# Gated linear attention: decay arguments of one direction from matrix products, both sides multiplied on VectorE, levels in groups of three

## The chip, the cores and the metric

The kernel runs on one core of one Trainium2 chip. Its time is the device time of one execution, in microseconds (us); three runs are given by their median.

## What is computed

The reference is a stack of two networks on 256 context and 256 latent tokens of width 1024. The part that the change touches is the gated linear attention mixer of the first layer: four heads of key width 128 and value width 256, run once forward and once backward over the 512 tokens.

```
q, k, v, g, a = split(h @ w_in)
logit = einsum('blzr,zrd->zbld', a.reshape(b, l, 2, 16), w_a2) + b_a2
log_a = log_sigmoid(logit) / 16
cum   = cumsum(log_a)                       # within a chunk
attn[i, j] = sum_d q[i,d] k[j,d] exp(cum[i,d] - cum[j,d])   for j <= i
o = attn @ v + (q * exp(cum)) @ state
state = state * exp(last) + (k * exp(last - cum))^T @ v
y = (rms_norm(o_forward + o_backward) * silu(g)) @ w_out
```

Since the decay differs in each key feature d, `attn` is no plain product. The kernel splits a chunk of 128 tokens by levels 64, 32, 16, 8, 4, 2, 1: at level s, queries and keys on the two sides of an edge between two runs of s tokens are scaled to that edge, which gives a plain product for the pairs that the edge parts. The exponents are differences between a running sum of log gates and its value at the edge.

## The kernel before, in words

Each stage is a block with one written-out program per engine (TensorE, ScalarE, GpSimd, VectorE, and SyncE for the loads), tied together by semaphores: `wait_ge` holds back the engine's whole queue, in order. Nothing is scheduled by a tool, so the order of the code is the order of the work. `b.stage()` begins a stage, with a barrier between stages.

`gla_project` makes queries, keys, values, gate and the log gates. Its TensorE program is long products in three parts (each weight slab is rounded on ScalarE, and the remainder is made on GpSimd). After eight short products (`logits`), ScalarE makes the softplus (`log_gate`, L1144), and VectorE forms the log gates and their running sums (`cum`), four forward and four backward, by scans.

`gla_core` is the stage of the change. For each of the four heads h it goes through levels n = 0 to 6 (sizes 64 to 1), q = 7h + n:

- VectorE makes the forward difference and GpSimd the backward one (`make_diff`, L1243), ScalarE takes four exponentials of 128x256 into `ak` and `bq` (`factors`, L1356 and L1357), VectorE multiplies the key side (L1516) and GpSimd the query side (L1440).
- TensorE multiplies them (`scores(h, n + 1)`, L1267, four products of 128x128), and VectorE takes the part that belongs to the level out of the bank with a mask (`take_score`, L1480). `scores(h, 0)` is the diagonal.
- Beside it run the state (`turn_keys` L1279, `addends` L1289, `states` L1502), the output of the head before (`outputs`, L1303 and L1308) and the sums of its squares (`add_squares`, L1062).
- TensorE also works off 40 *vector steps* (`ada_step`, L466; ten per head, spread by `STEPS`) that have nothing to do with the mixer: they multiply a stationary vector with two slabs of 512 KB each, which SyncE streams into a ring of four slabs. A load waits until the slab four places earlier has been used (`weights_used`), so at most two steps are loaded ahead.

A value in `[...]` of the order below is the list of semaphores that the instruction waits for.

## Time and profile before

| | us |
|---|---|
| median of 3 runs (2658.5 to 2662.23) | 2661.91 |
| profiled execution, its own time | 2668.94 |
| profiled execution, span | 2667.2 |
| `gla_core` in it | about 203.2 to 370.4 |
| TensorE busy over the span | 2481.5 (93%) |
| VectorE busy | 1360.4 (51%) |
| ScalarE busy | 1195.9 (45%) |
| GpSimd busy | 617.8 (23%) |

The span is from the first to the last instruction of the profiled execution, which took 0.3% more than the median of the three runs. The stage in question is 6% of it. A busy share over the whole span says little here, because stages have different limits; the heads of `gla_core` have to be read one by one. TensorE's float32 products appear as two records each, so a score product of four instructions shows as x8.

### The profile page before, as it was taken

To read this page: it belongs to the slowest core of one execution; us is meant where nothing else is said; L and a number is where in the kernel's file an instruction comes from. 1 tells how busy PE (TensorE), PEld (TensorE's weight loads), DVE (VectorE), ACT (ScalarE), POOL (GpSimd) and SP (SyncE) were. 2 spreads that over 40 slices of the span, in tenths; PEclk is the share of its full clock that TensorE was granted. 3 is DMA by queue.
4 is the path that set the end of the run, shared out by engine and by line. 5 is a ranking of instruction groups with operands and counts; after the bars stand their busy time and mean duration, and the time that the engine had idled before them with its cause. 6 is when DMAs were issued, how large, how long until landed. Compare 5 with 4: busy or idle time off the path is not lost. (4 is left out here: it accounts for less than half of the span.)

```text
span 2667.2 us, 35079 instructions
## 1 busy us (share of the span) xinstructions
PE 2481.5 (93%) x13744; PEld 1969.8 (74%) x13744; DVE 1360.4 (51%) x2129; ACT 1195.9 (45%) x2029; POOL 617.8 (23%) x376
## 2 busy tenths in 40 slices
PE   5997889999998998999997999999999979999988
PEld 3784457888888888578996767577767858768778
DVE  2207657433445666347665534552566444454665
ACT  1833334422327433455554345564366234565363
POOL 1437620000006434110001442003301116403310
PEclk8998999999999999988998999999999989999999
DMA  7236852333324332645764231222222323334333
GB/s 229 79 87 210 294 171 79 112 96 94 102 72 135 103 87 64 243 152 149 199 188 112 63 93 46 68 57 75 72 65 71 87 64 95 108 91 116 86 102 114
DMA packets 416683, 302.12 MB, mean 113 GB/s; under 512 B 10306, under 2 KB 388776, under 8 KB 416520
## 3 DMA queue, kind: packets, MB, share of 16 engines
q1 hardware_dynamic: 415408, 299.45, 38.3%
q8 instruction: 110, 1.80, 0.3%
q10 hardware_dynamic: 1112, 0.44, 0.1%
q14 instruction: 53, 0.43, 0.1%
HBM read 298.80 MB, written 1.05 MB: 112 GB/s over the span
## 5 line engine op out<-in xcount | busy, mean ns | idle before, releaser
L207 POOL TENSOR_TENSOR weights_lo<-wslots,weights_hi 128x1024 fp32r<-128x1024 f32 x158 | 386.6, 2455 | 868.7 <-ACT weights_hi L197 622.3
L197 ACT ACTIVATE weights_hi<-wslots 128x1024 fp32r<-128x1024 f32 x398 | 418.2, 1054 | 292.7 <-PE psum L260 235.0
L260 PE MATMUL psum<-input_hi,weights_hi 128*128 128x512 f32 (+1 forms) x1400 | 501.0, 358 | 4.5 <-PEq L831 1.8
L260 PE MATMUL psum<-input_hi,weights_lo 128*128 128x512 f32 (+1 forms) x1400 | 489.1, 349 | 0.0
L260 PE MATMUL psum<-input_lo,weights_hi 128*128 128x512 f32 (+1 forms) x1400 | 488.3, 349 | 0.0
L207 DVE TENSOR_TENSOR weights_lo<-wslots,weights_hi 128x1024 fp32r<-128x1024 f32 x240 | 296.4, 1243 | 187.7 <-ACT weights_hi L197 187.4
L260 PEld LDWEIGHTS psum<-input_hi,weights_hi 128*128 128x128 f32 x1400 | 264.5, 189 | 44.7 <-issue 7.5
L260 PEld LDWEIGHTS psum<-input_lo,weights_hi 128*128 128x128 f32 x1400 | 263.4, 188 | 39.2 <-issue 3.4
L260 PEld LDWEIGHTS psum<-input_hi,weights_lo 128*128 128x128 f32 x1400 | 263.7, 188 | 38.1
L260 PE MATMUL psum<-ffn_hidden_hi,weights_hi 128*128 128x512 f32 (+1 forms) x512 | 172.8, 338 | 0.0
L260 PE MATMUL psum<-ffn_hidden_hi,weights_lo 128*128 128x512 f32 (+1 forms) x512 | 172.5, 337 | 0.0
L260 PE MATMUL psum<-ffn_hidden_lo,weights_hi 128*128 128x512 f32 (+1 forms) x512 | 171.6, 335 | 0.0
L2304 DVE RECIPROCAL head_rstd<-head_rstd 128x512 f32<-128x512 f32 (+1 forms) x32 | 94.4, 2951 | 104.1 <-ACT head_rstd L2296 104.1
L3138 PE MATMUL psum<-input_hi,weights_hi 128*128 128x512 f32 (+1 forms) x384 | 139.4, 363 | 2.7 <-PEq L3225 2.7
L466 PE MATMUL psum<-wslots,ada_c 128*32 128x512 f32 x576 | 111.1, 640 | 27.2 <-DMA wslots<-ada_w 23.5
L3138 PE MATMUL psum<-input_lo,weights_hi 128*128 128x512 f32 (+1 forms) x384 | 133.0, 346 | 0.0
L3138 PE MATMUL psum<-input_hi,weights_lo 128*128 128x512 f32 (+1 forms) x384 | 132.7, 345 | 0.0
L279 PE MATMUL psum<-input_hi,weights_hi 128*128 128x512 f32 (+1 forms) x216 | 83.6, 387 | 48.2 <-DVE input_lo L684 44.6
L260 PEld LDWEIGHTS psum<-ffn_hidden_hi,weights_hi 128*128 128x128 f32 x512 | 96.8, 189 | 10.2 <-issue 0.2
L260 PEld LDWEIGHTS psum<-ffn_hidden_hi,weights_lo 128*128 128x128 f32 x512 | 96.5, 189 | 10.6
L260 PEld LDWEIGHTS psum<-ffn_hidden_lo,weights_hi 128*128 128x128 f32 x512 | 96.1, 188 | 11.2 <-issue 0.2
L997 ACT ACTIVATE ffn_hidden<-psum 128x512 f32<-128x512 f32 (+1 forms) x64 | 31.3, 490 | 135.9 <-PE psum L260 123.1
(449 smaller groups left out, 4864.7 us busy)
## 6 DMA issues: line engine op xcount, KB each, us to landing
wslots<-w_in SPq DMA_DIRECT2D x132, 512.0 KB, 3.9
wslots<-ffn_w SPq DMA_DIRECT2D x128, 512.0 KB, 4.1
wslots<-ada_w SPq DMA_DIRECT2D x96, 512.0 KB, 4.9
wslots<-ssd_w_in SPq DMA_DIRECT2D x49, 512.0 KB, 4.0
wslots<-w_ada SPq DMA_DIRECT2D x48, 512.0 KB, 4.6
wslots<-gla_w_in SPq DMA_DIRECT2D x25, 512.0 KB, 3.8
wslots<-w_br SPq DMA_DIRECT2D x24, 512.0 KB, 3.6
wslots<-ssd_w_out SPq DMA_DIRECT2D x16, 512.0 KB, 4.8
```

Of the source, the lines that this page charges most:

```text
L197: act.activation(self.part(self.whi_r, n), self.slot(n), ACT.Copy)\
L207: engine.tensor_tensor(self.part(self.wlo_r, n), self.slot(n), self.part(self.whi, n), ALU.subtract)\
L260: ins = pe.matmul(out_of(self.bank(g)), l, r, start=first and i == 0, stop=last and i == len(pairs) - 1, skip_group_check=not (first and l ...
L279: ins = pe.matmul(self.bank(g + j)[:, a:e], l, r, start=k == 0 and i == 0, stop=k == KD - 1 and i == 2, skip_group_check=True)
L466: ins = pe.matmul(b.psum[32 * q:32 * q + 32, bank, :], b.ada_c[:, blk, k, :], b.slot(n)[:, 0, q % 2 * 512:(q % 2 + 1) * 512], start=k == 0 ...
L997: act.activation(hid[:, j % NH, :], b.bank(g)[:, a:e], ACT.Relu).then_inc(b.reads_out(g), 1)
L2304: dve.reciprocal(r, r).then_inc(b.tick("dve_step"), 1)
L3138: ins = pe.matmul(b.bank(g)[:, a:e], w, u, start=x == 0, stop=x == len(pairs) - 1, skip_group_check=True)
```

## The change

- `gla_project`: the bias goes into the product as a row of ones (33 rows instead of 32), so the copy with bias (L1139) goes. The forward log gates stay as they are, tokens on partitions, with no scan; only the four backward ones are scanned. VectorE builds `sums`, nine 0/1 matrices of 128x128, one for each level and two for the chunk's ends, from a table of masks of 768 KB and one of 128 KB that are loaded at the stage's start.
- `gla_core`, forward side: the log gates are split into a rounded part and a remainder (`round_gates` on ScalarE, `split_gates` on VectorE, once per head). TensorE multiplies them with `sums` (`arguments(G, ...)`): three groups G of a head, each with three matrices (group 0 holds level 64 and the two ends, group 1 levels 32, 16, 8, group 2 levels 4, 2, 1), each in four *fills*, one per chunk of 128 tokens, of two products of 128x384. ScalarE takes one exponential of each fill (48 in all) into `decay`.
- `gla_core`, backward side: GpSimd makes all 32 differences (`make_diffs`), ScalarE the exponentials (`exponents_back`).
- VectorE multiplies both sides (`make_sides`, two instructions of 128x512 per level). GpSimd keeps the query factors of the chunk's ends and the small vectors.
- A level's sides wait for all four fills of its group. `STEPS` and the places of states, outputs and turns on TensorE are new; `addends(h, 2)` moves from the next head into its own.

```diff
+GLA_SIZES = [P // 2] + LEVELS
+GLA_SLOTS = len(GLA_SIZES) + 2
...
+                    sp.dma_start(wa[RB:RB + 1, z, :], d["gla_b_a2"][0, z:z + 1, :])\
+                        .then_inc(b.tick("gate_weights_in", 16), 16)
+                sp.dma_start(pairs[:], d["c_gla_masks"].rearrange("p (z n k) -> p z n k", z=2, k=P))\
+                    .then_inc(b.tick("pairs_in", 16), 16)
+                sp.dma_start(runs[:, 0:2, :], d["c_causal"]).then_inc(b.tick("pairs_in", 16), 16)
...
+                        pe.wait_ge(b.sem("log_gate_made"), b.nth("log_gate_made", n - 3))
+                    left, right = (wa[:, 1, i], aT[:]) if z else (aT[:, i], wa[:, 0, :])
+                    pe.matmul(b.psum[:, 4 + n % 4, :], left, right, start=True, stop=True)\
+                        .then_inc(b.tick("logit_ready"), 1)
...
-                    act.activation(lx[:, n % 2, :], b.psum[:, 4 + n % 4, :], ACT.Identity,
-                                         bias=column(b, C_GLAB, n)).then_inc(b.tick("logit_read"), 1)
...
-                for n in range(2 * GH):
-                    z, h = n // GH, n % GH
+                for n in range(2 * TT):
                     dve.wait_ge(b.sem("softplus_ready"), b.nth("softplus_ready", n + 1))
-                    dve.scalar_tensor_tensor(le[:, n % 2, :], lx[:, n % 2, :], 0.0, le[:, n % 2, :],
-                                                       ALU.min, ALU.subtract).then_inc(b.tick("dve_step"), 1)
+                    x = le[:, n % 2, :]
+                    ins = dve.scalar_tensor_tensor(x if n >= TT else b.H2[:, n, :], b.psum[:, 4 + n % 4, :], 0.0, x,
+                                                   ALU.min, ALU.subtract)
+                    if n >= TT:
+                        ins.then_inc(b.tick("dve_step"), 1)
+                        dve.wait_ge(b.sem("dve_step"), b.all("dve_step"))
+                        ins = dve.tensor_tensor_scan(b.H2[:, n, ::-1], reset[:], le[:, n % 2, ::-1], 0.0, ALU.mult, ALU.add)
+                    ins.then_inc(b.tick("log_gate_made"), 1)
...
+                step(dve.tensor_tensor(sums_r[:, 3:GLA_SLOTS, :], pairs[:, 0], blocks[:], ALU.mult))
...
-        STEPS = [1, 1, 1, 2, 2, 2, 1]
...
+        STEPS = (2, 1, 1, 2, 1, 1, 2)
+        EARLY = 2
...
+                    for c in range(first, last):
+                        f = G * FILLS + c
+                        if f >= 2:
+                            pe.wait_ge(b.sem("exponents_taken"), b.nth("exponents_taken", f - 1))
+                        for part, side in enumerate((gates_hi_r, gates_lo_r)):
+                            ins = pe.matmul(b.psum[:, ARG[c % 2], 0:WIDE * P], side[:, c, h * GDK:(h + 1) * GDK],
+                                            sums_r[:, g * WIDE * P:(g + 1) * WIDE * P], start=part == 0, stop=part == 1)
+                        ins.then_inc(b.tick("arguments_made"), 1)
...
+                scores(0, 0)
+                arguments(0, 0, FILLS)
+                vectors(0, 0, 0, EARLY)
                 for h in range(GH):
...
+                    G = h * GROUPS
+                    arguments(G + 1, 0, 1)
+                    if h:
+                        scores(h, 0)
+                        vectors(h, 0, 0, 1)
+                    arguments(G + 1, 1, 2)
+                    if h:
+                        outputs(h - 1)
+                    arguments(G + 1, 2, 3)
+                    scores(h, 1)
+                    if h:
+                        vectors(h, 0, 1, STEPS[0])
+                    arguments(G + 1, 3, 4)
+
+                    scores(h, 2)
+                    turn_keys(h, 0)
+                    arguments(G + 2, 0, 1)
+                    vectors(h, 1, 0, STEPS[1])
+
+                    scores(h, 3)
+                    turn_keys(h, 1)
+                    arguments(G + 2, 1, 2)
+                    vectors(h, 2, 0, STEPS[2])
+                    if h:
+                        sum_squares(h - 1)
+
+                    arguments(G + 2, 2, 3)
+                    scores(h, 4)
+                    vectors(h, 3, 0, STEPS[3])
+                    addends(h, 0)
+                    arguments(G + 2, 3, 4)
+
+                    scores(h, 5)
+                    addends(h, 1)
+                    arguments(G + 3, 0, 1)
+                    vectors(h, 4, 0, STEPS[4])
+                    if (h, 4) in TURN:
+                        turn_vectors(TURN[h, 4])
+
+                    scores(h, 6)
+                    addends(h, 2)
+                    arguments(G + 3, 1, 2)
+                    vectors(h, 5, 0, STEPS[5])
+
+                    arguments(G + 3, 2, 3)
+                    scores(h, 7)
+                    vectors(h, 6, 0, STEPS[6])
+                    arguments(G + 3, 3, 4)
+                    if (h, 6) in TURN:
+                        turn_vectors(TURN[h, 6])
...
+                def exponents(G, first, last):
+                    if G == GH * GROUPS:
+                        return
+                    if first == 0:
+                        buffer_free(G)
+                    for c in range(first, last):
+                        act.wait_ge(b.sem("arguments_made"), b.nth("arguments_made", G * FILLS + c + 1))
+                        act.activation(decay[:, G % 2, 0, :, c * P:(c + 1) * P],
+                                       b.psum[:, ARG[c % 2], 0:WIDE * P].rearrange("p (n k) -> p n k", k=P), ACT.Exp, scale=INV)\
+                            .then_inc(b.tick("exponents_taken"), 1)
...
+                            early, late = pairs(x, SIZES[0 if g == 0 else 3 * g - 2 + slot])
+                            act.activation(early, early, ACT.Exp, scale=INV)
+                            ins = act.activation(late, late, ACT.Exp, scale=-INV)
+                    ins.then_inc(b.tick("exponents_back"), 1)
...
+                    exponents(G + 1, 0, 2)
+                    exponents_back(G + 1, 0)
+                    if h:
+                        copy_output(h - 1)
+                    exponents(G + 1, 2, 4)
+                    exponents_back(G + 1, 1)
+                    exponents_back(G + 1, 2)
+                    vectors(h, 0)
+                    if h == 0:
+                        round_gates(1)
+                        round_gates(2)
+                        round_gates(3)
+                    else:
+                        square_output(h - 1)
+                    exponents(G + 2, 0, 1)
+                    copy_keys(h, 0)
+                    exponents_back(G + 2, 0)
...
+                    make_diffs(G + 1)
+                    pool.wait_ge(b.sem("exponents_taken"), b.nth("exponents_taken", (G + 1) * FILLS))
+                    pool.wait_ge(b.sem("exponents_back"), b.nth("exponents_back", (G + 1) * WIDE))
+                    if h >= 2:
+                        pool.wait_ge(b.sem("output_made"), b.nth("output_made", 2 * (h - 1)))
+                    for z in range(2):
+                        x = decay[:, G % 2, z, QUERY_SLOT, :]
+                        edge = x.rearrange("p (c r) -> p c r", r=P)[:, :, (P - 1) * (1 - z)]
+                        pool.tensor_copy(el[:, h % 2, z, :], edge).then_inc(b.tick("edge_copied"), 1)
+                        pool.tensor_tensor(qhT[:, h % 2, z, :], x, qT[:, h, :], ALU.mult).then_inc(b.tick("query_hat"), 1)
+                    if h:
+                        pool.wait_ge(b.sem("vectors_copied"), b.nth("vectors_copied", h))
+                        ada_finish(b, pool, h, vec)
+                    make_diffs(G + 2)
+                    make_diffs(G + 3)
...
+                    for z in range(2):
+                        if z == 0:
+                            dve.wait_ge(b.sem("exponents_taken"), b.nth("exponents_taken", (G + 1) * FILLS))
+                        else:
+                            dve.wait_ge(b.sem("exponents_back"), b.nth("exponents_back", G * WIDE + level_slot(n) + 1))
+                        x = decay[:, G % 2, z, level_slot(n), :].rearrange("p (n i s) -> p n i s", i=2, s=s)
+                        dve.tensor_tensor(crossed(sides[:, q % 2], z, s), x, crossed(qk[:, h], z, s), ALU.mult)\
+                            .then_inc(b.tick("sides_ready"), 1)
...
+                split_gates(0)
+                make_masks()
                 for h in range(GH):
                     for n in range(NL):
-                        q = h * NL + n
-                        if q + 1 < Q:
-                            make_diff(dve, 0, q + 1)
-                        if n == 3:
-                            key_hats(h)
-                        dve.wait_ge(b.sem("factors_ready"), b.nth("factors_ready", q + 1))
-                        x = ak[:, q % 2, :]
-                        dve.tensor_tensor(x, x, kT[:, h, :], ALU.mult).then_inc(b.tick("key_side"), 1)
-                        if q == 0:
-                            make_masks()
+                        if h or n:
+                            make_sides(h, n)
+                        else:
+                            take_score(0, 0)
+                            make_sides(0, 0)
                         if n == 0 and h:
                             take_score(h - 1, NI - 1)
-                        take_score(h, n)
-                        if n == 6:
-                            states(h, 0)
-                        if n in (0, 1) and h:
-                            states(h - 1, n + 1)
+                        if n or h:
+                            take_score(h, n)
+                        if n == 0:
+                            key_hats(h)
+                            if h == 0:
+                                for x in range(1, GH):
+                                    split_gates(x)
+                        if n in (4, 5, 6):
+                            states(h, n - 4)
...
```

How this moves the rows on the engines is shown at three places.

**TensorE, second head, around the product of level 32.** Before (`gla_bq` and `gla_ak` are the two sides; L466 is a vector step):

```order
L466 MATMUL psum<-wslots,ada_c 32x512
L1267 MATMUL psum<-gla_bq,gla_ak 128x128 [waits query_side,key_side,score_taken]
L1267 MATMUL psum<-gla_bq,gla_ak 128x128 x3
L466 MATMUL psum<-wslots,ada_c 32x512 [waits weights_in_3]
L466 MATMUL psum<-wslots,ada_c 32x512
```

Of the changed kernel, the same place (`gla_sums` are the 0/1 matrices, `weights_hi` and `weights_lo` hold the split log gates, `gla_sides` both sides; L468 is the vector step):

```order
L468 MATMUL psum<-wslots,ada_c 32x512 [waits weights_in_0]
L468 MATMUL psum<-wslots,ada_c 32x512
L1321 MATMUL psum<-gla_sums,weights_hi 128x384 [waits exponents_taken]
L1321 MATMUL psum<-gla_sums,weights_lo 128x384
L1334 MATMUL psum<-gla_sides 128x128 [waits sides_ready,score_taken]
L1334 MATMUL psum<-gla_sides 128x128 x3
```

The last fill of the group now stands directly ahead of the first score product that is made from this group.

**TensorE, same head, around the product of level 4,** of the changed kernel (L1365 are `addends`):

```order
L468 MATMUL psum<-wslots,ada_c 32x512 [waits weights_in_0]
L468 MATMUL psum<-wslots,ada_c 32x512
L1365 MATMUL psum<-gla_v,gla_kh 128x256 [waits key_hat_copied,output_copied]
L1365 MATMUL psum<-gla_v,gla_kh 128x256
L1321 MATMUL psum<-gla_sums,weights_hi 128x384 [waits exponents_taken]
L1321 MATMUL psum<-gla_sums,weights_lo 128x384
L1334 MATMUL psum<-gla_sides 128x128 [waits sides_ready,score_taken]
L1334 MATMUL psum<-gla_sides 128x128 x3
```

Here too the last fill (of group 2) and the first product of its levels are neighbours.

**VectorE, start of the stage.** Before:

```order
L1243 TENSOR_TENSOR gla_diff<-gla_cum 128x512 x2
L1516 TENSOR_TENSOR gla_ak<-gla_ak,gla_qk 128x512 [waits factors_ready]
L1463 TENSOR_SCALAR gla_masks<-half_ones 128x128 [waits masks_in]
L1465 TENSOR_TENSOR gla_masks<-gla_state 128x768
L1476 TENSOR_TENSOR gla_score<-psum,gla_diag 128x512 [waits score_made,masks_ready]
```

Of the changed kernel:

```order
L1638 TENSOR_TENSOR weights_lo<-h,weights_hi 128x4x128 [waits gates_rounded]
L1629 TENSOR_SCALAR gla_masks<-half_ones 128x128 [waits masks_in]
L1631 TENSOR_TENSOR gla_masks<-gla_state 128x768
L1662 TENSOR_TENSOR gla_score<-psum,gla_diag 128x512 [waits score_made,masks_ready]
L1652 TENSOR_TENSOR gla_sides<-gla_decay,gla_qk 128x4x2x64 [waits exponents_taken]
L1652 TENSOR_TENSOR gla_sides<-gla_decay,gla_qk 128x4x2x64 [waits exponents_back]
L1675 TENSOR_TENSOR gla_khT<-gla_decay,gla_qk 128x512 [waits exponents_back]
L1675 TENSOR_TENSOR gla_khT<-gla_decay,gla_qk 128x512
L1638 TENSOR_TENSOR weights_lo<-h,weights_hi 128x4x128 [waits gates_rounded] x3
L1652 TENSOR_TENSOR gla_sides<-gla_decay,gla_qk 128x8x2x32 [waits exponents_taken]
```

The sides of level 64 moved behind the masks, and the sides of level 32 stand behind three remainders, whose rounded parts ScalarE makes only after the exponentials of group 1.

## Rows read from the trace of the kernel before

**Rows 1.** Windows: the project stage's long part, then the four heads of the core.

```profile
core 0: us, PE busy (x) PEld busy (x) DVE busy (x) ACT busy (x) POOL busy (x), PEclk, DMA share, GB/s
...
120.00:203.00 83.00, 82.90 (x356) 66.42 (x354) 5.75 (x6) 33.61 (x43) 31.18 (x13) 1.00 0.29 83
...
203.00:249.20 46.20, 30.50 (x161) 15.18 (x160) 31.59 (x31) 17.67 (x47) 34.11 (x23) 0.78 0.63 221
249.20:287.00 37.80, 33.04 (x227) 19.51 (x225) 26.59 (x30) 15.50 (x43) 25.72 (x21) 1.00 0.79 268
287.00:324.20 37.20, 33.74 (x226) 19.34 (x225) 25.23 (x30) 15.49 (x43) 27.00 (x22) 1.00 0.80 288
324.20:370.40 46.20, 39.68 (x278) 25.57 (x276) 24.98 (x31) 14.39 (x40) 20.90 (x21) 1.00 0.77 258
```

**Rows 2.** Waits from 230 to 371: engine, line, releaser, us, times, longest.

```profile
POOL gla_bq L1440 <- ACT gla_bq L1357: 37.0, 13, 8.2
PEld psum L466 <- DMA wslots<-ada_w: 33.4, 30, 2.5
...
PE psum L1267 <- DVE gla_ak L1516: 2.4, 2, 1.2
```

**Rows 3.** Timeline of TensorE in the third head: start, duration, line, [idle before].

```profile
287.98 1.06 PE L1267 MATMUL psum<-gla_bq,gla_ak 128*128 128x128 f32 x8
288.87 0.60 PE L489 MATMUL psum<-ident,ada_flat 128*128 128x128 f32 x4
289.31 1.03 PE L1289 MATMUL psum<-gla_v,gla_kh 128*128 128x256 f32 x4
290.26 1.06 PE L466 MATMUL psum<-wslots,ada_c 128*32 128x512 f32 x8
...
295.42 1.06 PE L1303 MATMUL psum<-gla_score,gla_v 128*128 128x128 f32 x8
...
299.98 1.06 PE L466 MATMUL psum<-wslots,ada_c 128*32 128x512 f32 x8
...
302.15 0.60 PE L1279 MATMUL psum<-ident,gla_khT 128*128 128x128 f32 x4
302.68 1.06 PE L466 MATMUL psum<-wslots,ada_c 128*32 128x512 f32 x8
305.15 2.22 PE L466 MATMUL psum<-wslots,ada_c 128*32 128x512 f32 x8 [1.40 <-DMA wslots<-ada_w]
307.30 1.16 PE L1267 MATMUL psum<-gla_bq,gla_ak 128*128 128x128 f32 x8
308.29 0.60 PE L1279 MATMUL psum<-ident,gla_khT 128*128 128x128 f32 x4
...
315.15 1.84 PE L1062 MATMUL psum<-ones,gla_sq 128*128 128x1 f32 x16
316.93 2.19 PE L466 MATMUL psum<-wslots,ada_c 128*32 128x512 f32 x12
```

**Rows 4.** Timeline of the stage's start: masks on VectorE, first two level products.

```profile
209.73 1.84 DVE L1465 TENSOR_TENSOR gla_masks<-gla_state 128x768 uint8<-128x768 f32 x1
209.87 1.13 PE L1267 MATMUL psum<-gla_bq,gla_ak 128*128 128x128 f32 x8 [2.75 <-POOL gla_bq L1440]
...
214.79 2.05 PE L1267 MATMUL psum<-gla_bq,gla_ak 128*128 128x128 f32 x8 [3.79 <-DVE gla_ak L1516]
```

**Rows 5.** Groups by line, 230 to 371: busy us, mean ns | idle before.

```profile
L1480 DVE COPY_PREDICATED gla_score<-gla_masks,psum 128x512 f32<-128x512 uint8 x24 | 17.5, 731 | 32.0 <-PE psum L1267 31.8
...
L1356 ACT ACTIVATE gla_ak<-gla_diff 128x256 f32<-128x256 f32 x44 | 18.3, 416 | 46.5 <-PE psum L1267 23.9 <-DVE gla_diff L1243 19.8 <-POOL gla_diff L1243 2.9
...
L482 ACT ACTIVATE ada_flat<-psum 128x512 f32<-128x512 f32 x5 | 3.0, 597 | 27.2 <-PE psum L466 27.2
```

**Rows 6.** Timeline of VectorE and ScalarE in the third head.

```profile
302.45 1.76 DVE L1516 TENSOR_TENSOR gla_ak<-gla_ak,gla_qk 128x512 f32<-128x512 f32 x1
...
308.50 0.74 DVE L1480 COPY_PREDICATED gla_score<-gla_masks,psum 128x512 f32<-128x512 uint8 x1 [2.03 <-PE psum L1267]
308.58 0.44 ACT L1356 ACTIVATE gla_ak<-gla_diff 128x256 f32<-128x256 f32 x1 [1.32 <-PE psum L1267]
...
310.03 0.69 DVE L1516 TENSOR_TENSOR gla_ak<-gla_ak,gla_qk 128x512 f32<-128x512 f32 x1 [0.22 <-ACT gla_bq L1357]
```

376 lines of the change are left out of this document (208 added, 168 removed).

## The prediction

> **What bounds the kernel now.** I read first the windows of the stage, because over the span TensorE is 93% busy and tells nothing of one stage. In the long part of the project stage TensorE is busy for 82.90 of 83.00 us [rows 1]: what the change saves or adds there on the other engines is hidden behind it, or does not count. In the core the heads take 46.2, 37.8, 37.2 and 46.2 us, the last with the output of its own behind it [rows 1]. VectorE and GpSimd are busy for only 25 to 27 us of the two middle heads. Then the list of waits: GpSimd waits long for ScalarE (37.0 us), which costs nothing as long as TensorE does not wait for it. TensorE's queue of weight loads waits for the slabs of the vector steps (33.4 us in 141 us, some 9 per head) and hardly for a side of the scores (2.4 us) [rows 2]. So a middle head is TensorE's own work plus waits for slabs.
>
> TensorE's work follows from starts in the timeline of the third head [rows 3]: a score product 0.9 to 1.0 us (288.87 less 287.98, 308.29 less 307.30), a turn of keys 0.53, of vectors 0.45, addends 0.95, the outputs 4.6 (299.98 less 295.42), squares 1.8, a vector step 1.06. One head has 8 products (7.8), 2 turns (1.1), 3 addends (2.9), outputs, squares, a turn of vectors and 10 steps (10.6): 29.2 us. Against 37.2 that leaves 8.0 of waiting.
>
> The slabs explain most of it. The ring holds two steps, so a step cannot run before its slots, freed by the step two places earlier, are filled again. Step 3 of this head ends at 301.04, step 5 at 307.30 [rows 3]: 6.26 us, of which 1.06 are its own, so a refill takes about 5.2 us. I use 5.0 to 5.2. Where three pairs of steps stand close together (after levels 8, 4 and 2), the second of two has 2.7 us behind it and waits 2.4. Adding up this rule over the order of before gives 2.4 + 2.4 + 0.3 + 1.8 = 6.9 us of a head, most of the 8.0.
>
> **What the change adds to TensorE.** Per head 12 fills of two products of 128x384. The nearest row is the project stage, where a 128x512 product of the same rounded kind takes 83.00 / 356 = 0.233 us [rows 1]; three quarters of it is 0.175, so 0.35 a fill and 4.2 us a head. The bounds: as short as one of the eight records of a score product (0.12 each, 0.25 a fill, 3.0 a head), as long as the 512 columns (0.47, 5.6 a head). I take 0.35. Work per head: 33.4 us.
>
> **What it does to the waits for slabs.** The steps are now spread as 2, 1, 1, 2, 1, 1, 2, and one of the first two stands ahead of the outputs. I went through the new order with the same durations and the same refill of 5.0. Step 6 stands directly behind step 5 (squares, a fill and a product lie ahead of step 5): between the end of step 4 and step 6 lie 4.2 us, wait 0.9. Step 9: 0.3. Step 10: a fill, a product and step 9 lie between, 2.7, wait 2.3. The others have their 5 us. Sum 3.5, so the new order saves about 3.5 of 6.9, and the 1.1 that TensorE waited for other things goes too. Bounds: 0 and the old 7.
>
> **What it adds as a wait.** This term decides. In the shown order of TensorE the last fill of group 1 stands directly ahead of level 32's product, and the last fill of group 2 directly ahead of level 4's, and these products wait for `sides_ready`. Between the neighbours lies a chain over two engines, and nothing on TensorE can pass it: end of the fill to ScalarE 0.3 (308.29 to 308.58 [rows 6]); one exponential of 128x384 from a bank, 0.5 (between 0.416 for 256 columns and 0.597 for 512 [rows 5]); VectorE's two multiplications, 0.69 each when GpSimd is quiet (310.03 [rows 6]); 0.1 back. Together 2.3 us, twice per head: 4.6. Queued behind the product on TensorE are the turn of keys, the next fill and the next step, so the whole head moves. The slabs land meanwhile, but the steps that lack them (6 and 10) are not the ones behind these stalls, so little is given back. Bounds: with the exponential at 0.42 and hops of nothing it is 1.8 each; with both multiplications at 1.76, as beside a GpSimd instruction [rows 6], 4.4 each.
>
> A third place is short: the outputs wait for `take_score` of the head before, which on VectorE stands behind the two sides of level 64, which wait for the head's last fill. From that fill: 0.3 + 0.5 + 0.7 + 0.7 + 0.73 [rows 5] + 0.2 = 3.1, with GpSimd's query factors beside it up to 3.8. TensorE has a fill, a product, a step and a fill in front, 2.8. I take 0.6.
>
> The other levels: VectorE needs 0.73 + 1.4 = 2.1 between two sides, 3.1 where a state goes between; TensorE has 2.9 to 5 us of its own there. Nothing. ScalarE needs per head 12 x 0.5 + 7 x 0.83 + some 5 for copies, 17 of 42 us; GpSimd 8 differences and two products, about 14. Neither bounds.
>
> **Middle heads:** 33.4 + 3.5 + 4.6 + 0.6 = 42.1, against 37.8 and 37.2: +4.3 and +4.9.
>
> **Last head:** no fills for a next group (4 x 0.35 less), 40.7 to the end of its steps; then the last vectors are copied and turned (1.5), the outputs 4.6 and their copy 0.8: 47.6 against 46.2, +1.4. That `addends(h, 2)` moved is in it.
>
> **First head.** It is a chain of levels before: the products of levels 64 and 32 start at 209.87 and 214.79, after waits of 2.75 and 3.79, and the second already takes 2.05 instead of 1.06, with the mean granted clock of the head at 0.78 [rows 1, 4], that is partly at 1.2 GHz. Afterwards VectorE begins with the masks, whose table lands some 4 us into the stage; they end at 210 to 211 (209.73 + 1.84 before [rows 4]), then the diagonal and the sides of level 64, so that this product starts at about 213.5. Level 32 stands behind ScalarE's exponential of the last fill (0.5), four of 256 columns (1.7), three roundings (0.6 each), the last remainder (0.7) and two sides (1.4), with product, fill and hop 7.7 us: 221.3, 6.5 later than before. From there I count TensorE's order with its waits: 2.9, 3.3, then 8.7 (two steps short of slabs, and the stall), 3.4, 3.7 and 6.2, which ends at 249.5 against 249.2. The price is small because the old head was also slow in its middle; with some products at half clock I take +2. Bounds -3 and +6.
>
> **Project stage:** 0. ScalarE loses eight copies, VectorE four scans and gains some 25 short instructions, all beside the busy TensorE; 0.9 MB more on the queue of loads needs 3 us where it waits for GpSimd anyway.
>
> **Sum:** 2 + 4.3 + 4.9 + 1.4 = +12.6 us. On the profiled execution's 2668.94 that is 2681.5; on the median of the runs, 2661.91, it is 2674.5.
>
> **Rivals.** (A) *VectorE is slowed by GpSimd in the chain.* The same multiplication takes 0.69 alone and 1.76 in other places [rows 6]. If GpSimd's differences lie beside the chains, each of the four multiplications takes 1.07 more, and the outputs' chain 1.1: +5.4 a head, 22 in all, 2696. For it: VectorE has twice the multiplications. Against: GpSimd works a third of the head, and after the last fills its differences should be done. The Trainium skill (SBUF — State Buffer, on the shared port pair) says that a VectorE instruction with two SBUF inputs and a GpSimd instruction that reads SBUF exclude each other and the later one waits for all of the other; by that rule the sum would be (A)'s wherever the two meet, and the 12.6 where they don't. The trace agrees as to size, 1.76 against 0.69.
>
> (B) *The slabs are the only bound, and the new stalls hide in them.* If every slab lands during a stall, the 3.5 go too: heads of 38.6, in all 2 + 0.8 + 1.4 - 2.1 = +2.1, 2664, no change to be measured.
>
> (C) *Faster.* As (B), and the first head is no longer a chain of levels, since three levels come ready at once. It stands 8.7 us above a middle head today. If it falls to 40, -6, and with (B)'s others at +0.1, the time is 2656. It decides only if the product of level 32 starts before about 213; the wait for three roundings speaks against it.
>
> (D) *The fills don't run as assumed*, because changing between rounded and full products costs, or the clock falls in the stalls. At 0.47 a fill it is +5.8 in all, 2680, inside the range of the likeliest.
>
> **How the numbers follow.** Likeliest, with (D): 0.55, 2667 to 2684. (A) 0.15; (B) 0.13; (C) 0.17. A measurement of this kernel can tell about 0.2%, 5.3 us. Slower: 0.55 of the likeliest less 0.02, and (A): 0.68. Same: (B) and 0.02: 0.15. Faster: (C), 0.17. The range 2657 to 2700 leaves out half of (C) and the end of (A).
>
> **What would show it.** In the new profile: L1321 at about 0.17 us each; TensorE idle for 2 to 2.5 us before L1334 twice a head, released by VectorE's `gla_sides`; waits for `ada_w` at 3 to 5 us a head instead of 7 to 9; heads of about 42 us; VectorE's L1652 mostly at 0.7; level 32's first product near 221. It would be wrong if the score products after the last fills showed no idle time, if L1652 took over 1.2 us because of its crossed access (its runs are as short as one element, which no row of before shows on VectorE with two such operands), or if the ring refilled in 4 us.

## The result and the profile after

The changed kernel takes **2684.64 us** (median of 4 runs, 2682.94 to 2690.47), the kernel before beside it 2662.07 (4 runs). The ratio is 1.0078, 95% interval 1.0055 to 1.0102: the medians stand 22.6 us apart, where +12.6 was forecast. The time lies inside the stated range of 2657 to 2700, and 0.6 us over the upper end of the likeliest part (2684). The profiled execution took 2682.94 us, its span is 2681.2.

The windows of the four heads of the changed kernel, cut where each head's diagonal product starts, the first 0.9 us ahead of it at the stage's begin, and the last where its output ends (start:end, length, busy time and count on TensorE, its weight loads, VectorE, ScalarE, GpSimd, then granted clock, DMA share, GB/s):

```profile
203.90:254.07 50.17, 35.03 (x202) 20.05 (x203) 24.65 (x35) 19.39 (x45) 18.24 (x17) 0.93 0.59 205
254.07:298.46 44.39, 38.77 (x250) 24.39 (x249) 17.92 (x30) 14.64 (x38) 12.65 (x14) 0.92 0.68 237
298.46:342.76 44.30, 37.67 (x249) 24.62 (x249) 18.98 (x30) 15.09 (x38) 13.08 (x15) 0.96 0.69 236
342.76:392.10 49.34, 42.04 (x283) 27.68 (x282) 19.71 (x31) 13.67 (x35) 10.05 (x14) 0.97 0.73 238
```

Against [rows 1] the heads are 4.0, 6.6, 7.1 and 3.1 us longer, 20.8 in all. So the core holds nearly the whole difference of the medians. (The two profiled spans differ by only 14.0 us: behind the core the profile of before took 2294.0 us and this one 2286.3, in stages that differ from one execution to the next.) VectorE and GpSimd have less to do than before in both middle heads, and the granted clock of these, 1.00 before, is 0.92 and 0.96.

The waits of the changed kernel from 230 to 392 us (engine, line, releaser, us, times, longest), beside [rows 2]:

```profile
PEld psum L468 <- DMA wslots<-ada_w: 26.7, 21, 2.4
PE psum L1334 <- DVE gla_sides L1652: 14.5, 7, 2.1
PE psum L468 <- DMA wslots<-ada_w: 8.9, 13, 1.5
```

The slabs cost less than before (TensorE's own waits for them were 14.6 us in the 141 us of before, and are 8.9 in 162). The new line is the second: seven waits of 2.07 us for the two sides of a level. The timeline of TensorE in the third head shows one of them, around level 32's product, and the pair of steps behind level 8's:

```profile
308.28 0.45 PE L1321 MATMUL psum<-gla_sums,weights_hi 128*128 128x384 f32 x1
308.56 0.34 PE L1321 MATMUL psum<-gla_sums,weights_lo 128*128 128x384 f32 x1
310.97 2.05 PE L1334 MATMUL psum<-gla_sides 128*128 128x128 f32 x8 [2.07 <-DVE gla_sides L1652]
312.81 1.06 PE L1346 MATMUL psum<-ident,gla_khT 128*128 128x128 f32 x4
313.52 0.67 PE L1321 MATMUL psum<-gla_sums,weights_hi 128*128 128x384 f32 x1
313.99 0.51 PE L1321 MATMUL psum<-gla_sums,weights_lo 128*128 128x384 f32 x1
...
321.51 1.91 PE L468 MATMUL psum<-wslots,ada_c 128*32 128x512 f32 x12
324.18 1.05 PE L468 MATMUL psum<-wslots,ada_c 128*32 128x512 f32 x4 [0.75 <-DMA wslots<-ada_w]
```

ScalarE and VectorE meanwhile (same kernel, same place):

```profile
308.94 0.49 ACT L1474 ACTIVATE gla_decay<-psum 128x384 f32<-128x384 f32 x1 [1.81 <-PE psum L1321]
...
309.53 1.29 DVE L1652 TENSOR_TENSOR gla_sides<-gla_decay,gla_qk 128x512 f32<-128x512 f32 x2 [5.83 <-ACT gla_decay L1474]
```

Read together: the second product of the last fill starts at 308.56, and the next of its kind could have started 0.17 later, at 308.73; the exponential runs from 308.94, the two multiplications from 309.53 to 310.82, and the product starts at 310.97. That is the forecast chain link by link, 2.2 us from 308.73 against the forecast 2.3. (The profile lets the fill end at 308.90, so it shows 2.07 of idle time.) What the forecast did not have is behind it: the product takes 2.05 in place of 1.05, the turn of keys 1.06 in place of 0.60, the next fill 0.67 and 0.51 in place of 0.42 and 0.34. TensorE stood still for 2.07 us and then ran at the lower of its two levels (1.2 GHz; the granted clock is 0.51 from 310.97 to 314.42). From 310.97 to the next step at 314.42 pass 3.45 us; the same four groups take 1.85 at full clock (305.02 to 306.87 in run 1 below), so the clock costs 1.6.

Such stalls are not the only place. In the second head the clock is low behind level 32's product (0.56 from 266.11 to 270.00) and once more where no such stall stands ahead, behind the squares and level 8's product:

```profile
276.64:280.30 3.66, 3.56 (x15) 0.53 (x16) 0.00 (x0) 0.00 (x0) 0.00 (x0) 0.53 0.55 186
```

There two steps run that lack slabs, so what it costs can't be read off.

A middle head taken apart by the starts in TensorE's timeline (time from each group to the next, its own waits for slabs counted to the steps; us; worked out from all rows of the third head):

| | before | forecast | after |
|---|---|---|---|
| scores | 7.9 | 7.8 | 8.6 |
| turns, addends, outputs, squares | 10.6 | 10.8 | 9.9 |
| ten steps with slab waits | 17.6 | 14.1 | 15.1 |
| twelve fills | 0 | 4.2 | 6.6 |
| other waits | 1.1 | 5.2 | 4.1 |
| head | 37.2 | 42.1 | 44.3 |

### The profile page after: what moved, and what is told of

Same layout as the page of the kernel before. It is cut to its first block and busy times, and to the rows that moved or that the text cites. A ratio compares the mean times of both kernels' runs of the same rounds, so it can differ in the third digit from the quotient of the medians.

```text
span 2681.2 us, 35271 instructions
## 1 busy us (share of the span) xinstructions
PE 2486.5 (93%) x13840; PEld 1977.0 (74%) x13840; DVE 1338.5 (50%) x2154; ACT 1191.9 (44%) x2001; POOL 561.0 (21%) x353
## 3 DMA queue, kind: packets, MB, share of 16 engines
HBM read 299.72 MB, written 1.05 MB: 112 GB/s over the span
## 5 line engine op out<-in xcount | busy, mean ns | idle before, releaser
L262 PE MATMUL psum<-input_hi,weights_hi 128*128 128x512 f32 (+1 forms) x1400 | 500.5, 357 | 4.4 <-PEq L833 1.8
L262 PE MATMUL psum<-input_hi,weights_lo 128*128 128x512 f32 (+1 forms) x1400 | 488.3, 349 | 0.0
L262 PE MATMUL psum<-input_lo,weights_hi 128*128 128x512 f32 (+1 forms) x1400 | 487.3, 348 | 0.0
L262 PEld LDWEIGHTS psum<-input_hi,weights_hi 128*128 128x128 f32 x1400 | 263.8, 188 | 44.8 <-issue 7.8
L262 PEld LDWEIGHTS psum<-input_lo,weights_hi 128*128 128x128 f32 x1400 | 263.8, 188 | 39.2 <-issue 3.4
L262 PEld LDWEIGHTS psum<-input_hi,weights_lo 128*128 128x128 f32 x1400 | 263.9, 188 | 38.1
L262 PE MATMUL psum<-ffn_hidden_hi,weights_hi 128*128 128x512 f32 (+1 forms) x512 | 172.0, 336 | 0.0
L262 PE MATMUL psum<-ffn_hidden_hi,weights_lo 128*128 128x512 f32 (+1 forms) x512 | 171.7, 335 | 0.0
L262 PE MATMUL psum<-ffn_hidden_lo,weights_hi 128*128 128x512 f32 (+1 forms) x512 | 170.8, 334 | 0.0
L468 PE MATMUL psum<-wslots,ada_c 128*32 128x512 f32 x576 | 104.5, 631 | 21.4 <-DMA wslots<-ada_w 17.6
L262 PEld LDWEIGHTS psum<-ffn_hidden_lo,weights_hi 128*128 128x128 f32 x512 | 96.1, 188 | 11.2 <-issue 0.2
L262 PEld LDWEIGHTS psum<-ffn_hidden_hi,weights_hi 128*128 128x128 f32 x512 | 96.6, 189 | 10.2 <-issue 0.2
L262 PEld LDWEIGHTS psum<-ffn_hidden_hi,weights_lo 128*128 128x128 f32 x512 | 96.1, 188 | 10.6
```

The source lines that it names most:

```text
L262: ins = pe.matmul(out_of(self.bank(g)), l, r, start=first and i == 0, stop=last and i == len(pairs) - 1, skip_group_check=not (first and l ...
L468: ins = pe.matmul(b.psum[32 * q:32 * q + 32, bank, :], b.ada_c[:, blk, k, :], b.slot(n)[:, 0, q % 2 * 512:(q % 2 + 1) * 512], start=k == 0 ...
```

## The experiments

The runs of one kernel lie some 15 us apart (the kernel before beside runs 9 to 12: 2657.44 to 2672.6), and the stages behind the core, which no edit touches, take 2279.6 to 2299.8 us in the 14 profiles. The medians of the kernel before beside the runs below are 2665.87 (runs 1 to 4), 2666.36 (5 to 8) and 2667.28 (9 to 12), 4 to 5 us above the 2662.07 of its four runs beside the changed kernel. Against these medians the changed kernel stands 17 to 19 us higher, not 22.6. Beside the ratio, a second measure is therefore given: the length of the core in the profile, from the first diagonal product to the first product of the next stage that reads the squares (`gla_stat`). It is 169.05 us in the profile of before and 190.09 in that of the changed kernel (204.79 to 394.88), +21.0. Two profiles of the kernel before agree in it to 0.3 (run 12). A core figure below is of one profile, and "less" is against the changed kernel where nothing else is named.

**1. The last fill of group 1 earlier.**

```diff
-                    arguments(G + 1, 2, 3)
+                    arguments(G + 1, 2, 4)
                     scores(h, 1)
                     if h:
                         vectors(h, 0, 1, STEPS[0])
-                    arguments(G + 1, 3, 4)
```

> Edit: the changed kernel, with the last fill of group 1 one product and one vector step earlier, ahead of level 64's product. Theory T (stalls count in full, and the low clock behind level 32's product comes from the stall): the 2.07 us of idle time before that product fall to 0 to 0.3, the product takes 1.05 in place of 2.05, and the three later heads are 4 us shorter each, the first about unchanged: about 2684.6 - 12 = 2672.5 us. Rival S (slab waits take over what a stall frees): waits for ada_w rise from 5 to 8 or 9 us a head, the time falls by under 4 us, above 2680. Rival C (the low clock there is not the stall's doing): idle time goes, the product stays at 2.05, about -6, 2678.5.

Measured: 2675.43 us, ratio 1.0038 (1.0023 to 1.0053); core 178.99, 11.1 less than the changed kernel. Middle heads 40.28 and 41.57. Level 32's product of the third head, in this kernel:

```profile
305.02 1.13 PE L1334 MATMUL psum<-gla_sides 128*128 128x128 f32 x8 [0.36 <-DVE gla_sides L1651]
```

The wait is 0.36 and the product at full clock in all three later heads. Three times 1.71 of idle time went. Of the other 6 us of the 11.1, some 3 are clock (1.6 each in the second and the last head; the third loses as much as before, at another place); the rest is small pieces: steps that wait 0.2 to 0.6 less a head, the fill that now follows another fill, 0.5 in the first head. Theory T holds, and S and C fall: the freed time was not taken by the slabs, and the low clock behind this product went with the stall. The third head still has a granted clock of 0.96, now behind the stall of level 4, whose product takes 1.29.

**2. The last fill of group 2 earlier.** The same edit two levels on: `arguments(G + 2, 2, 4)` ahead of `scores(h, 4)`, and the call behind `addends(h, 0)` removed.

> Edit: the changed kernel, with the last fill of group 2 ahead of level 8's product, two vector steps and one pair of addends, so that these cover the chain to level 4's product. Theory T: 2.07 us of idle time less in each of the four heads and no change of clock, since the product behind this stall was already at 1.13: -8, 2676.5 us. Rival S: under -3, above 2681.5, because steps 7 and 8 then wait for slabs.

Measured: 2674.43, ratio 1.0032 (1.0008 to 1.0055); core 177.36, 12.7 less. That is more than the 8.3 of four stalls. Most of the rest is clock (1.6 us each in the second and the last head, behind level 32's product), in a place where I had not expected it. Level 32's products, whose stall is untouched here:

```profile
264.64 1.13 PE L1334 MATMUL psum<-gla_sides 128*128 128x128 f32 x8 [2.07 <-DVE gla_sides L1651]
...
304.22 1.43 PE L1334 MATMUL psum<-gla_sides 128*128 128x128 f32 x8 [2.07 <-DVE gla_sides L1651]
```

So the same stall of 2.07 us is followed by the low clock in one head (304.22, then 1.06 for the turn) and not in the others. In the changed kernel, with two stalls in a head, all three later heads lost clock. With one stall (this run and the one ahead of it) one middle head of two did, and with none, below, neither.

**3. Both earlier.**

> Edit: both of the other two, the last fill of group 1 ahead of level 64's product and the last of group 2 ahead of level 8's. Theory T: the gains add, -20, 2664.5 us, with middle heads of 38.3 and waits for ada_w still at 5 us a head. Rival S: they don't add, since the ring of slabs then bounds (10 steps of at least 2.6 us plus bunching): middle heads of 41 and more, above 2672. Rival V (VectorE's chain of levels takes over): no idle time released by a fill's chain, but by sides elsewhere, VectorE busy over 85% of a head.

Measured: 2663.58, ratio 0.9995 (0.998 to 1.001); core 170.44, 19.65 less. The two middle heads:

```profile
250.00:287.76 37.76, 35.20 (x249) 23.29 (x249) 17.96 (x30) 14.53 (x38) 12.64 (x14) 1.00 0.77 273
287.76:326.34 38.58, 36.33 (x250) 23.25 (x250) 19.03 (x30) 14.88 (x38) 13.08 (x15) 1.00 0.77 273
```

The clock is 1.00, and 19.65 of the 21.0 us that the change added to the core are gone with two lines of TensorE's program. In the last head the clock is still low once, over the last turn and part of the outputs (0.96 over that head). The twelve fills take 5.6 us here, 0.47 each, in place of 6.6. S and V fall.

**4. The roundings and remainders of heads 1 to 3 later in the first head.** ScalarE's `round_gates(1)` goes behind `copy_keys(h, 0)`, 2 and 3 behind `copy_keys(h, 1)`; on VectorE:

```diff
                             key_hats(h)
-                            if h == 0:
-                                for x in range(1, GH):
-                                    split_gates(x)
+                        if h == 0 and 0 < n < GH:
+                            split_gates(n)
```

In the changed kernel the three remainders stood ahead of level 32's sides on VectorE, and behind three roundings:

```profile
217.63 3.19 DVE L1638 TENSOR_TENSOR weights_lo<-h,weights_hi 128x512 fp32r<-128x512 f32 x3 [1.57 <-ACT weights_hi L1457]
220.74 1.28 DVE L1652 TENSOR_TENSOR gla_sides<-gla_decay,gla_qk 128x512 f32<-128x512 f32 x2
```

> Edit: the changed kernel, with the roundings and remainders of heads 1 to 3 moved behind level 32 to level 8 of the first head, so that they don't stand ahead of level 32's sides. Theory T: VectorE's three remainders (3.2 us from the first to the last) and ScalarE's roundings (1.65) leave the chain to level 32's first product; it starts 3 us sooner, near 219 on the clock of the profile, and the time falls by 3, 2681.5 us, all in the first head. Rival: the low clock of this head stays as it is and something else of the chain comes last (GpSimd's differences, the exponentials), under -1, 2684.

Measured: 2688.39, ratio 1.0089 (1.0059 to 1.0118); core 188.10, 2.0 less, the first head 0.8 less. The product does start 2.8 us sooner after the head's begin, but the time does not follow: theory T's 3 us are not there, and the rival's "under 1" fits the first head. VectorE, and then GpSimd, of this kernel show why it gains little:

```profile
215.23 2.35 DVE L1676 TENSOR_TENSOR gla_khT<-gla_decay,gla_qk 128x512 f32<-128x512 f32 x2
218.13 2.62 DVE L1653 TENSOR_TENSOR gla_sides<-gla_decay,gla_qk 128x512 f32<-128x512 f32 x2 [0.54 <-ACT gla_decay L1474]
...
226.09 0.69 DVE L1639 TENSOR_TENSOR weights_lo<-h,weights_hi 128x512 fp32r<-128x512 f32 x1 [4.69 <-ACT weights_hi L1457]
226.69 1.28 DVE L1653 TENSOR_TENSOR gla_sides<-gla_decay,gla_qk 128x512 f32<-128x512 f32 x2
```
```profile
217.72 3.93 POOL L1581 TENSOR_TENSOR gla_decay<-h 128x512 f32<-128x512 f32 x3 [1.28 <-DVE gla_khT L1676]
```

Two multiplications that take 1.28 alone take 2.62 beside GpSimd's three differences: rival (A)'s mechanism, for once, in the only head where the two engines meet in a chain. The Trainium skill (SBUF — State Buffer, section on the two separate sides) says that such a pair excludes each other for a whole instruction. The trace agrees in size: the pair of multiplications takes 1.34 longer, and one of GpSimd's three differences takes 1.31. And at 226.09 the remainder now waits for its late rounding and holds level 16's sides. The queue was moved, not removed.

**5. The steps one at a time, stalls kept.** Of the ten steps, one stands after the diagonal, one in the middle of the outputs, one behind them, and one after each level:

```diff
                        ins.then_inc(b.tick("output_made"), 1)
+                        if h < GH - 1:
+                            vectors(h + 1, 1 + vt, 0, 1)
...
-        STEPS = (2, 1, 1, 2, 1, 1, 2)
+        STEPS = (1,) * 10
...
```

> Edit: the changed kernel with its ten vector steps of a head one at a time (after level 128's product, in the middle of the outputs, behind them, then after each level's product) and no pair of steps left; the last fills of groups 1 and 2 stay where the change put them, so both stalls of 2.07 us stay. Theory T (slab waits of some 4 to 5 us a head come from steps that stand close together, a refill being 5.1 us, and add to the stalls): waits for ada_w fall under 1.5 us a head, middle heads from 44.3 to 41, the time to 10 us over the kernel before. Rival S (the ring's rate, not the bunching, sets the waits): under 1 us a head, 20 us over the kernel before.

Measured: 2672.11, ratio 1.0031 (1.0012 to 1.005); core 183.75, 6.3 less. The profiled execution was its slowest (2692.55). The third head is 40.97 long, with no wait for slabs, as theory T said. The second is 44.52: it waits 1.3 us for a slab once, and the clock is low twice, behind the squares (the step at 282.09 takes 2.51 to the next start in place of 1.00) and behind level 4's stall (the product takes 1.67, the addends 1.35 in place of 0.68). Behind its stall at level 32 the product takes 1.13, at full clock. In the third head the waits for slabs were worth what was expected; in the second the clock and one late slab took all of it back.

**6. Steps, fills and start together.**

> Edit: the steps one at a time as in the spread kernel, both last fills ahead of the product before theirs, and the roundings and remainders of heads 1 to 3 later in the first head. Theory T: work of a head 29.2 + 12 fills at 0.44 = 34.5, no stall but 0.4, slab waits under 1: middle heads of 35.5 to 36, against 37.8 with both fills ahead alone; the time 12 to 16 us under the kernel before, ratio 0.995. Rival V (VectorE's and ScalarE's chain of levels then sets the pace): idle time before the scores at other levels, heads of 37 and more, no better than both fills ahead alone.

Measured: 2646.52, ratio 0.9936 (0.9913 to 0.996); core 151.53. Middle heads 34.35 and 35.02, the first 39.76. Better than expected, and V falls. What I had not expected is the first head, 6.4 us shorter than in run 3 (46.17): the third and fourth step now stand where TensorE waits for levels 64 and 32, in place of behind them.

**7. What a fill's second product costs.** On run 3, each fill is one product in place of two. The kernel leaves out the remainder's part of the forward arguments:

```diff
-                        for part, side in enumerate((gates_hi_r, gates_lo_r)):
+                        for part, side in enumerate((gates_hi_r,)):
...
```

> Edit: both last fills ahead, and each fill made of one product in place of two; left out is the remainder's part of the forward arguments. It measures what a fill's second product costs on the path. Theory T (TensorE's work is the head's length; a fill's second product has a pitch of 0.17 to 0.18 us): 12 x 0.175 = 2.1 us a head, -8 against both fills ahead alone. Rival S (the slabs take over what TensorE saves): the waits for ada_w grow by as much, under -3.

Measured: 2664.21, ratio 0.9992 (0.9976 to 1.0008), no less than run 3. In the profile the core is 164.70, 5.7 less than run 3; the fills take 3.5 us a head in place of 5.6 (the 2.1 expected), of which 0.35 come back as a longer wait before level 32 (0.71) and some as slab waits. The 5.7 us are not seen in the time. The two ratios differ by 0.0003, 0.8 us, with some 6 us either way: that leaves T's 8 just outside and S's 3 inside, while the core lies between them, so this run does not decide.

**8. Run 3 with the later roundings.**

> Edit: both last fills ahead, and the roundings and remainders of heads 1 to 3 later in the first head; the steps stay in pairs. It tells in the combined kernel the share of the start from that of the steps. Level 32's first product starts 2.8 us sooner after the head's begin, as in the start kernel alone, but levels 16 and 8 then wait for VectorE's sides, so the first head gains 0.8 and the time stands 0 to 2 us under both fills ahead alone. Rival: the gain stays in full, -3.

Measured: 2667.78, ratio 1.0008 (0.9993 to 1.0023); core 168.89, 1.5 less than run 3. The time is as expected, but the gain is not where it was expected: the first head takes 46.33 against 46.17, and the last is 1.8 us shorter, where in run 3 the outputs ran at low clock and here they don't. The start by itself is worth nothing.

**9. The kernel before, with its steps one at a time.** The same placing of the steps in the old order; nothing else of the change.

> Edit: the kernel BEFORE the change, with its ten vector steps of a head one at a time (one after level 128's product, one in the middle of the outputs, one ahead of the squares, and so on), nothing else of the change. It tells what the new scheme of arguments is worth once both orders are free of waits for slabs. Theory T (a head is TensorE's own work plus slab waits): 29.2 of work and 1 to 2 left of slab waits, middle heads 31 to 32 against 37.5, the time 18 to 22 us under the kernel before (ratio 0.992 to 0.993), level with or better than the spread form of the changed kernel. Rival V (the old scheme's chain of a level over GpSimd, ScalarE and VectorE cannot go faster than some 5 us a level): idle time of 1 us and more before the score products, heads of 35 to 36, the time 5 to 10 us under the kernel before, and the new scheme keeps an advantage.

Measured: 2655.98, ratio 0.9958 (0.9939 to 0.9977); core 156.90, 12.2 less than before. Neither theory: the middle heads, 37.05 and 33.38, did not reach 31 to 32, but no chain of a level stood in their way either (idle time outside the steps 0.2 and 1.2 us). The first head still has 8.5 us of waits for the sides of levels 64, 32 and 16. The second lacks slabs twice (2.4 us), and behind the squares and the second of these waits the clock is low, with no stall of a chain ahead (0.53 from 279.30 to 282.90; 0.95 over the head). The third head:

```profile
284.83:318.22 33.39, 32.18 (x229) 19.62 (x225) 25.57 (x30) 15.54 (x43) 26.65 (x22) 1.00 0.89 308
```

The DMA share is 0.89 at 308 GB/s. The head's ten steps need 20 slabs of 512 KB, 10.5 MB, and at 308 GB/s that is 34 us. That the ring's own rate is the next bound is likely and not shown: four of the ten steps are stretched, to 1.4 to 1.9 us, but a share of 0.89 is not full, and no run has another ring.

**10. The steps one at a time and both fills ahead, roundings left.**

> Edit: the changed kernel with the steps one at a time and both last fills ahead, but the roundings and remainders of heads 1 to 3 where the change put them. Against the run that had all three it tells what the start is worth once steps fill its waits. Theory T: level 32's first product waits 2.8 us longer, of which the steps before it hide part; the first head 41 to 42.5 in place of 39.8, the time 1.5 to 2.5 us over the kernel with all three. Rival (the 6.6 us by which that first head was shorter came from the start edit after all): first head near 46, +6.

Measured: 2640.27, ratio 0.9904 (0.9878 to 0.993); core 151.40, the same as run 6. The first head is 38.99, not longer. So the 6.4 us of that head came from the steps, and the edit of the start gave nothing; both the theory's 1.5 to 2.5 and the rival's 6 were wrong. One middle head of this kernel:

```profile
278.49:313.24 34.75, 34.53 (x250) 23.29 (x250) 19.02 (x30) 14.90 (x38) 13.08 (x15) 1.00 0.87 301
```

TensorE is busy for 34.53 of 34.75 us. Twelve fills take 5.3 us here, 0.44 each.

**11. The masks behind level 64's sides, the last outputs ahead of the last turn.** On top of run 6.

> Edit: the kernel with all three (steps one at a time, last fills ahead, roundings later), and in addition the masks made behind level 64's sides in place of ahead of them, and the last outputs ahead of the last turn of vectors. Expected of the masks: 1 to 1.8 us off the start of the chain of levels in the first head, of the outputs' order 0.8 us at the end: 1 to 2.5 us under the kernel with all three (17 to 22 under the kernel before, ratio 0.993). Rival: slabs for the first head's third and fourth steps come no sooner, so the start gains nothing.

Measured: 2642.52, ratio 0.991 (0.9892 to 0.9927); core 149.86, 1.7 less than run 6. The core agrees with the sum that was expected, 0.5 of it in the first head (1 to 1.8 expected of the masks) and 1.1 in the last (0.8 expected of the outputs); between runs 6, 10 and 11 the times cannot tell.

**12. The kernel before again.**

> The kernel before, unchanged, for a second profile of it. Question: the granted clock of the project stage behind the logits (82 to 90 and 110 to 124 us) was 1.00 in the one profile of before and 0.76 to 0.88 in one or both stretches in seven of nine profiles of the changed kernel and its variants. If the change's arguments lowered it, it is 1.00 here too; if it comes and goes in either kernel, 0.9 or less can show here. Middle heads should be 37 to 38 again, with no product of a level above 1.2 us in them.

Measured: one run, 2653.61; core 168.79. Its middle heads are 37.41 and 38.89, with no slow product. Two windows of the project stage, first of the changed kernel, then of this run; in each of them four of the eight small products of the logits end (L1131, two records each; 33 rows, before 32):

```profile
82.00:90.00 8.00, 8.00 (x23) 5.04 (x22) 0.69 (x1) 7.46 (x10) 1.91 (x1) 0.79 0.15 56
110.00:124.00 14.00, 14.00 (x49) 9.97 (x48) 3.83 (x4) 13.47 (x16) 5.84 (x2) 0.88 0.15 43
```
```profile
82.00:90.00 8.00, 8.00 (x27) 4.70 (x27) 0.85 (x2) 6.74 (x9) 0.00 (x0) 1.00 0.24 69
110.00:124.00 14.00, 14.00 (x56) 10.21 (x55) 3.83 (x4) 13.77 (x18) 6.15 (x3) 1.00 0.26 75
```

And TensorE's timeline of the changed kernel in the second of them, where such a product of L262 takes 0.39 to 0.40 at full clock:

```profile
109.11 3.70 PE L1131 MATMUL psum<-gla_a,gla_wa 33*128 33x512 f32 x8
112.73 0.62 PE L262 MATMUL psum<-weights_hi,input_hi 128*128 128x512 f32 x1
```

In the changed kernel 49 records fit where 56 fit before. In all, one or both windows were below 1.00 in 8 of 11 profiles of the changed kernel and its variants and in none of the three profiles of the kernel before (with run 9). At 0.79 of 8 us and 0.88 of 14 it costs 1.7 us in each window (3.4 in run 8, where the second is at 0.76). The core's first product starts at 203.19 to 204.86 in the three profiles of the new scheme without it, at 204.79 to 207.27 in the eight with it, and at 203.43 to 204.45 in the three of the kernel before. That the change brings it is likely, three profiles against eleven being few, but no run separates the logits' new form from the rest of the change, and the cause stays open.

## Why the prediction was right, and by how much it was short

The direction and the range held, and so did the mechanism that decided; the sum was 12.6 and the measurement 22.6 (17 to 19 against the later medians of the kernel before). The third head came out nearer than its terms: fills, scores and steps are 2.4, 0.8 and 1.0 over the forecast, the other groups and waits 0.9 and 1.1 under it, and that these offset each other is luck.

- **The stall before levels 32 and 4** was the deciding term, and it was right: 2.2 us forecast as 2.3, twice a head, link by link, and runs 1 to 3 took it away with one call each.
- **The clock behind the stall** has no term in the sum, and is one of the two things that were missing most from a later head. The prediction named it under (D) only as a way for the fills to cost more. It costs 1.6 us where it falls behind level 32's product; run 1, which took three stalls of 1.71 net away, gave back 11.1, some 3 of it clock. It is not tied to these stalls alone: it was also low behind the squares (second head of the changed kernel and of runs 5 and 9).
- **The fills** were taken at 0.35 each, by scaling the project stage's 512 columns. The twelve take 6.6 us in the third head, 0.4 of it clock: 0.52 each, over the upper bound of 0.47. The first of the two products starts its second 0.28 later (308.28, 308.56), and behind turns and addends a fill takes 0.53 to 0.63. The 0.175 holds inside a run of rounded products and not where a fill follows a product of full float; put in pairs, fills take 0.47 (run 3) and 0.44 (run 10). This is the other thing missing, and the term that was mis-sized most: 2 us a head.
- **The slab waits**: before, 17.6 less 10.6 = 7.0 (forecast 6.9); after, 15.1 less 10.6 = 4.5 (forecast 3.5). The refill held: from issue to landing a slab takes 4.9 us in the median, in both kernels. The pair behind level 8 waits 1.5 rather than 0.9. Half of that is idle time (0.75, before 324.18). The other half is in the step itself: with both slabs there, its eight records take 1.00 from start to next start (314.42); where the second slab is late, its four records alone take 0.98 (324.18 to 325.16). The prediction counted a late step at 1.06, although its own row of step 5 showed 2.22 [rows 3].
- **The outputs' wait** of 0.6 does not exist: no idle time stands before them in any of the three heads.
- **The first head** was forecast to start levels 64 and 32 at 213.5 and 221.3; they start at 213.82 and 222.17. It grew by 4.0 rather than 2.
- **The project stage** was put at 0; in the profile it lost some 3 us of clock, see run 12, yet the core starts only 0.7 us later than before (204.79 against 204.13).
- **Rival (A)** falls for the later heads: L1652 takes 0.684 in the median of its 42 instructions there. It lives only in the first head (run 4). **(B)** falls: run 1 gave back all of the stall, so it hid no slab wait. **(C)** needed level 32's product before 213; it came at 222. Its first head of 40 can be had, but not by (C)'s mechanism: in runs 6 and 10 it is 39 to 40 because steps fill its waits. The sign "L1652 over 1.2 us" did not show, but the crossed access has a price at one level: 1.10 in place of 0.68 at level 1, see the last section.

The question behind the change, whether the new arguments are worth their fills, has its answer in runs 9 and 10. With the steps one at a time in both, the core takes 156.9 us in the old scheme and 151.4 in the new, one profile each; the medians are 11 and 27 us under the kernel before, so only 5.5 of the 15.7 us between them are seen in the core. The third heads are 33.4 against 34.75: the fills' 5.3 us stand against 4.0 that the other groups and waits take less (steps 1.45, waits 1.0, scores 0.8, the rest turns, addends and outputs). The new scheme wins in the first head (39.0 against 43.3), where the old one waits for GpSimd and VectorE level by level, and in the second (34.7 against 37.05), where the old one lacks slabs and clock. The change itself was sound, and its order cost it nearly everything: 19.65 of 21.0 us in the core.

## What to carry to other kernels

When producer and consumer of a chain over other engines stand side by side in TensorE's order, the chain counts in full; put one or two independent groups of its own length between them before judging the scheme. Price a stall with the clock behind it: here 2.07 us of stillness cost up to 1.6 us more, behind three of its seven stalls of this length. A stream with a short ring of buffers wants its consumers evenly spaced, and those consumers are then the natural filler for the waits.

## What the hardware showed that was not expected

- The same stall of 2.07 us was followed by products at the low clock in some heads (2.05 for four products of 128 columns, eight records) and not in others (1.13). Of the second and third heads, those with two stalls had a granted clock of 0.92 or 0.96, with one stall 1.00 or 0.96, and those of the new scheme with none 1.00 in all six profiles. In the old scheme with its steps one at a time (run 9) the second head had 0.95 without such a stall.
- A 384-column product of rounded operands behind a product of full float took 0.26 to 0.36 us to the next start, one behind another rounded product 0.17.
- TensorE busy without a gap can lose clock too: behind four products of 33 rows (eight records) that take 3.70 us, the next eight products of 128x512 took 0.62 to 0.63 us each where 0.39 to 0.40 is usual.
- VectorE's multiplications with the crossed access took 0.67 to 0.69 us for 512 columns in the later heads as long as its runs were two elements or more. At level 1, where they are one element, each took 1.07 to 1.11, with GpSimd idle. The first of the pair in the third head of the changed kernel:

```profile
332.35 1.10 DVE L1652 TENSOR_TENSOR gla_sides<-gla_decay,gla_qk 128x512 f32<-128x512 f32 x1
```

- A vector step writes four strips of 32 rows from two slabs. With both slabs there it took 1.00 us; with the second slab late, each half took about as long as the whole (0.98 to 1.05).
